# Attention with the values stationary and the turned probabilities moving

## The reference

```python
def diff_attend(q, k, v, lam):
    s = jnp.einsum('bqhmd,bkhmd->bhmqk', q, k).astype(jnp.float32) * (DA_QK ** -0.5)
    p = jax.nn.softmax(s, axis=-1)
    a = p[:, :, 0] - lam * p[:, :, 1]
    return jnp.einsum('bhqk,bkhv->bqhv', a.astype(v.dtype), v)
...
    s = (jnp.einsum('bqhd,bkhd->bhqk', q_nope, k_nope)
         + jnp.einsum('bqhr,bkr->bhqk', q_rope, k_rope)).astype(jnp.float32) * MLA_SCALE
    p = jax.nn.softmax(s, axis=-1)
    return jnp.einsum('bhqk,bkhv->bqhv', p.astype(v.dtype), v)
```

## Time and profile before

| | us |
|---|---|
| median of 3 runs | 1423.97 |
| lowest, highest run | 1418.46, 1428.31 |
| span of the profiled execution | 1417.9 |
| PE busy in it | 1172.4 (83%) |
| DVE busy | 463.5 (33%) |
| ACT busy | 266.9 (19%) |
| POOL busy | 122.1 (9%) |

### The profile page before, as it was taken

The page is one execution under the profiler, slowest core; times in us unless marked ns, Lnnn a source line. Parts: engine busy times, 40 slices in busy tenths (PEclk is TensorE's granted clock), DMA queues, the critical chain, the costliest instruction groups (busy, mean ns, idle before and its releaser), DMA issues.

```text
span 1417.9 us, 15930 instructions
## 1 busy us (share of the span) xinstructions
PE 1172.4 (83%) x6032; PEld 567.1 (40%) x6032; DVE 463.5 (33%) x1121; ACT 266.9 (19%) x592; POOL 122.1 (9%) x107
## 2 busy tenths in 40 slices
PE   5899978878989599999985499986799699995553
PEld 2363433444654333333332447432468333332222
DVE  5111456764742611111101421357663511110003
ACT  1220101223530411111101322001251311110002
POOL 2000031820000010000000200033200100000001
PEclk9999999979899799999998699997689799997776
DMA  9622106739996389999999401006003689999972
GB/s 337 242 86 93 60 0 261 289 131 412 374 353 274 140 326 372 389 390 395 395 399 397 187 4 56 0 0 237 0 1 119 252 313 385 388 410 413 407 327 93
DMA packets 86997, 344.03 MB, mean 243 GB/s; under 512 B 6918, under 2 KB 42187, under 8 KB 64395
## 3 DMA queue, kind: packets, MB, share of 16 engines
q1 hardware_dynamic: 67728, 309.68, 56.5%
q10 hardware_dynamic: 15195, 19.86, 4.1%
q0 software_dynamic: 4000, 13.49, 2.7%
HBM read 300.92 MB, written 42.07 MB: 242 GB/s over the span
## 4 chain that ended last, share of the span: by engine, by line
PE 61%; DMA 20%; DVE 11%; ACT 3%; issue 2%; SPq 1%; POOL 1%; ACTq 0%; POOLq 0%; DVEq 0%
PE ps L901 13%; PE ps L503 12%; DMA ring<-in_exp_w_up 10%; PE ps L924 6%; PE ps L791 6%; PE ps L512 5%; PE ps L446 4%; DMA ring<-in_w_mod 3%; DMA slots<-arena 2%; PE ps L468 2%; DMA arena<-in_exp_w_up 2%; PE ps L688 2%; PE ps L770 2%; PE ps L668 2%; PE ps L740 1%
## 5 line engine op out<-in xcount | busy, mean ns | idle before, releaser
L901 PE MATMUL ps<-ring,arena 128*32 128x256 f32 (+1 forms) x1344 | 197.8, 534 | 45.1 <-DMA ring<-in_exp_w_up 45.1
L503 PE MATMUL ps<-u,ring 128*128 128x512 f32 (+1 forms) x416 | 168.0, 564 | 9.5 <-ACT u L1743 4.0
L446 PE MATMUL ps<-cst,arena 128*128 128x128 f32 x558 | 110.3, 318 | 65.7 <-DVE arena L1445 33.0
L446 PEld LDWEIGHTS ps<-cst,arena 128*128 128x128 f32 x558 | 70.2, 160 | 172.0 <-issue 81.5
L901 PEld LDWEIGHTS ps<-ring,arena 128*32 128x32 f32 (+1 forms) x1344 | 71.3, 136 | 154.4 <-issue 146.5
L1601 DVE TENSOR_TENSOR arena<-arena,ps 128x128 f32<-128x128 f32 (+1 forms) x59 | 27.3, 503 | 317.3 <-ACT arena L1903 317.3
L503 PEld LDWEIGHTS ps<-u,ring 128*128 128x128 f32 x416 | 80.0, 194 | 94.9 <-issue 90.1
L901 PE MATMUL ps<-arena 128*64 128x512 f32 (+1 forms) x544 | 82.2, 528 | 17.6 <-DMA arena<-in_exp_w_up 17.6
L924 PE MATMUL ps<-arena 128*32 128x256 f32 (+1 forms) x672 | 94.4, 485 | 1.6 <-ACT arena L1912 1.6
L791 PE MATMUL ps<-u,ring 128*128 128x512 f32 (+1 forms) x256 | 83.6, 487 | 2.3 <-DVE h L1426 1.3
L512 PE MATMUL ps<-ring,u 128*128 128x256 f32 (+1 forms) x224 | 76.6, 502 | 7.7 <-DVE arena L1245 7.7
(11 more groups left out here) (291 smaller groups left out, 1221.9 us busy)
## 6 DMA issues: line engine op xcount, KB each, us to landing
ring<-in_w_mod SPq DMA_DIRECT2D x24, 2048.0 KB, 10.9
ring<-in_exp_w_gate SPq DMA_DIRECT2D x22, 2048.0 KB, 18.6
ring<-in_exp_w_up SPq DMA_DIRECT2D x22, 2048.0 KB, 23.0
arena<-in_exp_w_down SPq DMA_DIRECT2D x22, 2048.0 KB, 20.1
slots<-zeros SPq DMA_DIRECT2D x4, 6144.0 KB, 41.9
arena<-in_exp_w_gate SPq DMA_DIRECT2D x10, 2048.0 KB, 20.7
u<-in_exp_w_down SPq DMA_DIRECT2D x10, 2048.0 KB, 19.7
arena<-in_exp_w_up SPq DMA_DIRECT2D x10, 2048.0 KB, 26.7
```

The lines of the kernel that those rows point to most:

```text
L446: return nc.tensor.transpose(dst, src, ident[0:n, 0:n])
L503: last = nc.tensor.matmul(bank[row:row + width, 0:T - c0], w[:, k, n:n + width], u[:, k, c0:T], start=(k == 0), stop=(k == KT - 1))
L901: last = nc.tensor.matmul(ps[n * part:n * part + n, 2 + b % 2, 0:2 * width].rearrange("p (s n) -> p s n", s=2), x_k, pair[:, :, a:a + widt ...
```

## The change

Units alternate between da and ml. The scores' scale moves into the evacuations of q, the maximum is negated as it is written, and da and ml scores have banks of their own (2 and 3, and 4). The value products are turned round: 64 columns of values are the weights, 128 columns of turned probabilities move, and the result has features on partitions, two heads side by side in the partition halves of a bank. They are issued for two units of a kind at once, in turn for either half. The ml maps are scaled on POOL before they are turned. The norm's mean square comes from a product with a block matrix of ones, so that its root lies beside the result, and one DVE operation applies gain, factor and root as it places. The result's transposes, DVE's copy, square, sum and scaling are gone.

```diff
-LAG_OUT, LAG_NORM, LAG_TURN, LAG_PLACE = 7, 8, 9, 10
+HEAD_UNITS = 2 * DA_H
+LAG_PV, LAG_SQUARE, LAG_MEAN, LAG_ROOT, LAG_ML, LAG_DA = 3, 10, 10, 11, 11, 12
...
-            for t in range(0 if layer == 0 else NCTX // P, TT) for kind in ("da", "ml") for hh in range(DA_H)]
+            for t in range(0 if layer == 0 else NCTX // P, TT) for hh in range(DA_H) for kind in ("da", "ml")]
...
+def tile_part(layer, s, lag):
+    i, rest = divmod(s - lag, HEAD_UNITS)
+    return i if rest == 0 and 0 <= i < len(attention_units(layer)) // HEAD_UNITS else None
...
+def pairs_done(n):
+    return 4 * (n // HEAD_UNITS) + 2 * (n % HEAD_UNITS // 4) + n % 2 + 1
...
+        def scores_of(kind):
+            return ps[:, 2:4, :] if kind == "da" else ps[:, 4:5, :]
+        def heads_of(kind):
+            return ps[:, 0 if kind == "da" else 1, 0:256]
...
@@ PE
                         if kind == "da":
-                            pe.wait_ge(S("mixed"), before // 2 + sum(1 for x in units[:n + 1] if x[0] == "da"))
+                            pe.wait_ge(S("mixed"), before + n + 1)
                         else:
-                            pe.wait_ge(S("exp_done"), before + n + 1)
+                            pe.wait_ge(S("ml_scaled"), (before + n) // 2 + 1)
...
-                    n = s - 3
-                    if 0 <= n < len(units):
+                    n = s - LAG_PV
+                    if 0 <= n < len(units) and n % 4 >= 2:
...
                         for k in range(nk // P):
-                            last = nc.tensor.matmul(ps[:, g % 2, 64 * hh:64 * hh + 64], probs_t[:, n % 2, k, :],
-                                                    v[:, k, 64 * hh:64 * hh + 64], start=(k == 0),
-                                                    stop=(k == nk // P - 1))
+                            for unit in (n - 2, n):
+                                hh = units[unit][2]
+                                r, c = 64 * (hh % 2), P * (hh // 2)
+                                last = nc.tensor.matmul(heads_of(kind)[r:r + 64, c:c + P],
+                                                        v[:, k, 64 * hh:64 * hh + 64], probs_t[:, unit % 4, k, :],
+                                                        start=(k == 0), stop=(k == nk // P - 1),
+                                                        tile_position=(0, r))
...
+                    i = tile_part(l, s, LAG_MEAN)
+                    if i is not None:
+                        pe.wait_ge(S("lam_sums"), l + 1)
+                        pe.wait_ge(S("o_squared"), units0 // HEAD_UNITS * l + i + 1)
+                        nc.tensor.matmul(ps[:, 5, 0:256], head_ones, o_sq, start=True,
+                                         stop=True).then_inc(S("o_means"), 1)
...
@@ DVE
-                emptied(v.tensor_copy(qk[:, m, c0:T], claim(f"qk{l}{m}")[:, 0:T - c0]))
+                emptied(ts(qk[:, m, c0:T], bank, DA_SCALE, None, ALU.mult) if m < 2 else
+                        v.tensor_copy(qk[:, m, c0:T], bank))
...
-                        link(v.tensor_reduce(mx[:, s, 0:nm], ps[:, pair:pair + nm, 0:nk], AX.X, ALU.max))
-                        ts(nb[:, s, 0:nm], mx[:, s, 0:nm], -(DA_SCALE if kind == "da" else MLA_SCALE), None,
-                           ALU.mult).then_inc(S("max_ready"), 1)
+                        v.tensor_reduce(nb[:, s, 0:nm], scores_of(kind)[:, :, 0:nk], AX.X, ALU.max,
+                                        negate=True).then_inc(S("max_ready"), 1)
+                    for kind, lag in (("ml", LAG_ML), ("da", LAG_DA)):
+                        i = tile_part(l, s, lag)
+                        if i is not None:
+                            place_heads(l, kind, i)
...
+            def place_heads(l, kind, i):
...
+                if kind == "da":
+                    dve.wait_ge(S("o_root"), tiles_back + i + 1)
+                    placed = stt(u[:, 0:2, P * t:P * t + P], heads, vec[:, l, V_SUBG:V_SUBG + 1],
+                                 o_root.rearrange("p (m n) -> p m n", n=P), ALU.mult, ALU.mult)
                 else:
+                    dve.wait_ge(S("heads_done"), 4 * tiles_back + pairs_done(HEAD_UNITS * i + 7))
+                    placed = v.tensor_copy(u[:, 6:8, P * t:P * t + P], heads)
...
@@ ACT
+                    i = tile_part(l, s, LAG_SQUARE)
+                    if i is not None:
+                        act.wait_ge(S("heads_done"), 4 * tiles_back + pairs_done(HEAD_UNITS * i + 6))
...
+                        a(o_sq, heads_of("da"), ACT.Square).then_inc(S("o_squared"), 1)
+                    i = tile_part(l, s, LAG_ROOT)
+                    if i is not None:
+                        keep = (1.0 - lam_init(l)) ** 2
+                        act.wait_ge(S("o_means"), tiles_back + i + 1)
...
+                        rsqrt(o_root, ps[:, 5, 0:256], S("o_root"), 1.0 / (DA_V * keep), small[:, 21 + l:22 + l])
...
@@ POOL
+            def attention(l):
+                rr = stats[:, 2]
+                for n, (kind, _, _, nk) in enumerate(attention_units(l)):
+                    if kind == "ml":
+                        pool.wait_ge(S("mixed"), units0 * l + n + 1)
+                        part = probs[:, n % 3, 0, 0:nk]
+                        g.tensor_scalar(part, part, rr[:, n, 0:1], None, ALU.mult).then_inc(S("ml_scaled"), 1)
```

More of the change, by code:

```diff
@@ L1358, in attention @@
                         else:
[L1359 removed]
+                            v.reciprocal(rr[:, n, 0:1], rs[:, n, 0:1]).then_inc(S("mixed"), 1)
                     spare(mod_in_attention(l, s))
[L1361 to L1364 removed]
@@ L1622, in _ @@
             v.memset(small[:, 20:21], EPS)
+            for l in range(DEPTH):
+                v.memset(small[:, 21 + l:22 + l], EPS / (1.0 - lam_init(l)) ** 2)
             link(v.memset(cond[:, :, :], 0.0))
```

127 lines of the change are left out of this document (46 added, 81 removed).

## The result

| | before | changed |
|---|---|---|
| median of the timed runs (six each), us | 1420.44 | 1433.12 |
| lowest, highest | 1418.46, 1428.31 | 1430.75, 1438.48 |
| ratio to before, 95% interval | | 1.0091 [1.0065, 1.0118] |
| span of the profiled execution, us | 1417.9 | 1436.7 |
| mean granted clock | 0.896 | 0.883 |

What follows compares the result with a forecast made beforehand. The prediction took PE, DVE and ACT work in the two attention stretches as the bound. Layer 1's -2.4 and layer 0's -8.0 sum to -10.4: 1417.9 becomes 1407.5 profiled, 1413.5 against the 1423.97 median; range 1405 to 1426.

Steps and rivals of the forecast that it cites:

- What bounds the kernel: Both attention stretches: savings in layer 1, and in layer 0 behind 348.8, should reach the end one for one.
- GpSimd's multiply 1.04 us: Scaling each ml map between DVE's reciprocal and PE's transposes: 1.04 us, bounds 0.5 and 1.5, plus 0.1 for hand-overs.
- Value products overlap: PE's 16 value-product records for two units overlap across output halves: 0.90 us instead of 1.68.
- third rival: Value products don't overlap, or GpSimd takes over 2 us beside DVE; the order's gain is eaten: 1424, chance 0.14.
- Period of 5.0 us: Attention at full clock: one da and one ml unit together take 5.0 us instead of 5.5.
- the loop's 9.6: Path through all engines from one da maximum to that two pairs later: 9.6 us, so 4.8 per pair.
- No wait above 0.9, so no fall of the clock in layer 0: Layer 0 attention: no PE wait longer than 0.9 where the clock fell before, so no fall counted; before, 13.4 us ran at half speed.
- first rival: Layer 0's clock falls as before; 13.4 us at the lower level give 4.5 back: about 1418, chance 0.17.
- Alternation evens out the engines: Attention units alternate da, ml, because four of one kind in a row leave first PE and then DVE idle.
- The tail of 7.9 (7.5 in layer 0): End of attention, from the last scores' end to the output projection: 7.9 us, 7.2 before; 7.5 in layer 0.
- The fourth: Clock stays at 1.2 GHz in both layers' attention, a pair costs 7.5 instead of 5.0: about 1443, chance 0.09.
- second rival: GpSimd is cheap (0.6) and layer 1's clock rises 10 us sooner: 1407, chance 0.20.

Runs made afterwards that it cites:

- e1: Changed kernel without GpSimd's multiply of the ml maps, results left unscaled, for timing only: 0.9969 of the kernel before.
- e3: Changed kernel with the ml map scaled on DVE directly behind its reciprocal, nothing on GpSimd: 0.9959 of the kernel before.
- e12: Changed kernel with GpSimd's multiply issued as a product of two tensors, the reciprocal broadcast, instead of a scalar per partition: 1.0017 of the kernel before.
- e11: Changed kernel with ml scaling on DVE and ACT's copy of unit s-2 ahead of the exponential of unit s: 0.9926 of the kernel before, 1409.5 us.
- e9: Changed kernel with ml scaling on DVE and idle, unread products added where PE would wait: 0.9970 of the kernel before.
- e10: Changed kernel with units in the old order, four da then four ml, scaling still on GpSimd: 1.0011 of the kernel before.
- e15: Changed kernel with units in the old order, four da then four ml, and ml maps scaled on DVE: 0.9955 of the kernel before.
- e7: Kernel before with only idle, unread products added, ahead of 512-key da transposes and near layer 1's start: 0.9993 of the kernel before.
- e4: Changed kernel with idle, unread products of 256 columns added ahead of the transposes that wait longest: 1.0004 of the kernel before.

## Why the prediction was wrong

- **What bounds the kernel: right.** Whatever a variant saved in layer 1 or behind the last modulation piece came out at the end: the middle and the end of all profiles agree within 4 us, with nothing new in them. Layer 1's clock rose 22 us after the first maximum, 23 before, as the forecast took it, and the eighth unit's scores had begun by then. It did not count on this time being so movable (8 to 9 us in e1 to e3).
- **GpSimd's multiply 1.04 us: wrong.** It took 1.56, outside the bounds of 0.5 and 1.5. The nearest row was sought by width and by what is computed, and it had two tensors as operands; the instruction has one tensor and a scalar for each partition. e12 gives this step 10.5 us of the miss. The Trainium skill (GPSIMD Engine Reference, Engine selection) gives one-input operations about the speed of DVE and calls two-input ones about twice as slow. For this size the traces don't agree with the first: 1.56 with one tensor, against DVE's 0.49 for the same multiply. With two tensors it is 1.04, against DVE's 0.69.
- **Value products overlap: right.** Sixteen records take 1.02 us in the chain at the full clock, 0.9 forecast, 1.7 if they didn't overlap. At the lower level they take 1.9. The third rival called every value product a change of the tiling mode; but the sixteen of a group have one shape and change only the half, so there is one such change a group, and the 0.12 above the forecast is, as an estimate, what it can have cost.
- **Period of 5.0 us: sized too low.** In the changed kernel two pairs from one da maximum to the next took 11.4 us (385.54 to 396.92, all at the full clock), against 10.0 forecast: the loop's 9.6, 0.2 for mean and placing, 0.2 for DVE and GpSimd hindering each other. The chain of waits shows the terms:

```profile
385.54 1.13 DVE arena L1371
...
386.84 1.57 POOL arena L2042
388.45 0.66 PE ps L466 x4
389.11 1.02 PE ps L792 x16
390.13 1.06 PE ps L756 x4
391.19 0.59 PE ps L466 x4
391.78 1.02 PE ps L792 x16
392.80 0.63 PE ps L801 x2
393.43 0.87 PE ps L759 x2
394.33 0.69 DVE arena L1371
395.02 0.33 DVE u L1402
```

  GpSimd is 0.5 above its term, two sets of transposes 1.25 instead of 0.88 (0.44 was the distance between starts, when the next product follows at once; ahead of a unit that reads the transposes' result it is the whole length), two sets of value products 2.04 instead of 1.80. The mean product (0.63, priced at 0.43) and a placing (0.33) lie in the chain once in four pairs, and the other placing (0.39, at 398.06) in the next two pairs: 0.34 a pair, where 0.1 was counted. With the falls of the clock the last four pairs of layer 1 took 30.0 us (1049.8 to 1079.8), 7.5 each.
- **No wait above 0.9, so no fall of the clock in layer 0: wrong, and by estimate the largest term.** It failed first at the very place for which it was worked out: at the first 512-key units PE waited 1.81 us for ACT's copy (364.18), where it had waited 1.54 before, and the clock fell for 4 us. The forecast had found that ACT "isn't late" from its load of 3.6 us in a period of 5.0, and not from its order: the copy stands behind the exponentials, and e11, with the copy first, has no such wait.

  It failed again in the loop, where the prediction's own sum contradicts it. With a period of 5.0 and 3.76 of work for PE, two pairs leave 2.5 us in which PE must wait; with the pass at the forecast price (e12) two waits of 1.2 stood at a fall of 10 us. e12 took 64.7 us in layer 0 where 52.9 were forecast. Of its 21 us at the lower level some 17 were not in the forecast; by the rate in the prediction's first rival (13.4 us cost 4.5) they are an estimated 6 of the 12. The terms just named, with a longer tail, make up the rest.

  For the changed kernel the two stretches took 131.3 us where 104.2 were forecast, and some 40 us more at the lower level than was counted; by the same rate they are an estimated 14 of these 27. The stretch from 390 to 398 in the earlier trace rows that "held its clock" at 78% busy was no evidence for this loop: none of its waits was over 0.83.
- **Alternation evens out the engines: wrong.** It was to give most of 5.0 against 5.5 us. Under equal conditions it gave 0.9959 against 0.9955. What the variants of the change gain comes from its other parts, the turned value products and DVE's smaller load among them, which were not told apart.
- **The tail of 7.9 (7.5 in layer 0): too short.** From the end of the last scores to the projection it took 1091.26 - 1079.76 = 11.5, and 11.5 in layer 0 too: transposes, value products (3.68) and mean product (1.22) ran at the lower clock, 3 us more than counted, and GpSimd's pass was 0.5 longer.
- **The rivals.** The fourth named the mechanism (PE waits a fifth of each period and the clock stays down) and the sign, at 0.09. It came true in part: 47 us of layer 1 at the lower level (23 of them as before), but only spells of 3.5 to 7 us in layer 0 behind 358. Its 1443 was 10 above the time. The third had "GpSimd takes over 2 us" as one way to 1424; a pass of 1.56 sufficed to add 10.5 us, an estimated half of it in clock. The first rival's mechanism came too, since 17 us of layer 0's attention did run at the lower level; its 1418 was 15 short, because it changed nothing else. The second rival's earlier rise in layer 1 came in variants alone.

What stays open: which waits bring the clock down. The falls inside the attention that were read stand at a wait of PE, but not every wait brings one: 1.34 didn't in layer 0 of the changed kernel, and 1.35 did in its layer 1; 1.81 for ACT's copy did in the changed kernel and in e12, and didn't in e1 and e3. How the 19.6 us of the miss divide between the pass and the clock stays an estimate too: taking the pass away gives 1.2% and filling the waits 0.9%, and with the scale on DVE the filling adds nothing (e9), so the two shares overlap. PE's timeline at the same four da units of e10 and of e15:

```profile
387.57 0.66 PE L467 MATMUL ps<-cst,arena 128*128 128x128 f32 x4 [1.65 <-DVE arena L1387]
388.15 1.09 PE L793 MATMUL ps<-arena 128*64 128x128 f32 x16
```

```profile
384.60 0.71 PE L467 MATMUL ps<-cst,arena 128*128 128x128 f32 x4 [1.65 <-DVE arena L1387]
385.25 1.98 PE L793 MATMUL ps<-arena 128*64 128x128 f32 x16
```

The wait is 1.65 in both; the clock stayed in the first and fell in the second, though PE had been busier ahead of it there. What the fall costs is read from the lengths; when it comes was not settled. Nor does less of the lower clock always mean less time: e15 has 50 us of it in the two stretches and e3 22, and their ratios are equal.

## What to carry to other kernels

Subtract each engine's work from the period that you forecast: the remainder is waiting, it falls in pieces that can be written down, and for TensorE a piece of a microsecond or more may cost as much again in clock (behind a wait of 1.74, transposes, value products and scores took an estimated 1.5 us longer). An engine's load tells that it can keep up, and its order tells whether a result is late: compare both. Price an instruction of an engine by a row of the same form (operands, scalar or tensor), not only of the same size. A stage handed to an idle engine is free only if its result is early; ask what stands ahead of it in the giving engine's order, and after removing a wait look at the next engine's order, which here gave 0.3% on top of 0.4 (0.9959 to 0.9926 by ACT's copy ahead of its exponential).

## What was not expected of the hardware

- GpSimd multiplied 128x512 in 1.56 us by a scalar for each partition (256 columns 0.92) and in 1.04 us by the same scalar as a broadcast tensor (256 columns 0.61).
- Products that nobody reads made the changed kernel 0.9% faster (1.0091 to 1.0004), by granted clocks of .94 and .86 in the two stretches against .85 and .64.
- At the lower level four transposes took 1.12 us for 0.66, sixteen records of value products 1.97 for 1.09, four records of da scores 2.08 for 1.13.
- The clock rose between 2 and 23 us after layer 1's first maximum, by variant (2 to 3 in e7, 8 to 9 in e1 to e3, 15 to 16 in e4 and e12, 22 to 23 in the two kernels).
